# Weight remainders written over the loaded weight blocks: one ring of six slots, 74 pages, in a two-layer block stack on one core

## What is computed

```python
for l in range(DEPTH_2):
    h = rms_norm(x, ln_mix_pre[l])
    proj = h @ w_in[l]
    c_q, c_kv, k_pe, conv_u, r_q, r_k, r_v, r_g, gate_logits = jnp.split(proj, points, axis=-1)
    ...
    y_conv = conv_branch(conv_u, conv_w_dw[l], conv_b_dw[l], conv_ln_g[l], conv_ln_b[l], conv_w_pw[l])
    ...
    gates = jax.nn.sigmoid(gate_logits).reshape(B, S, N_BRANCH, D_MODEL)
    merged = gates[:, :, 0] * y_mla + gates[:, :, 1] * y_conv + gates[:, :, 2] * y_ret
    x = x + rms_norm(merged @ w_out[l], ln_mix_post[l])
    ...
def conv_branch(u, w_dw, b_dw, ln_g, ln_b, w_pw):
    a, gate = jnp.split(u, 2, axis=-1)
    a = a * jax.nn.sigmoid(gate)
    ...
    y = jax.nn.silu(layer_norm(y, ln_g, ln_b))
    return y @ w_pw
```

## Time and profile before

| | |
|---|---|
| median of 3 runs | 2887.31 us (2887.26 to 2887.69) |
| the profiled execution | 2887.51 us, its span 2885.5 us |
| granted TensorE clock, mean | 0.996 |
| PE busy | 2813.1 us, 97% of the span |
| DVE, ACT, POOL busy | 1284.7, 1136.1, 1193.7 us (45, 39, 41%) |
| DMA | 96 GB/s mean, 277.97 MB |

### The profile page before, as it was taken

One profiled execution on the slowest core, in us unless ns is written; L12 is line 12 of the kernel. 1 busy time (PEld: TensorE's weight loads), 2 busy tenths in 40 slices (PEclk: granted clock), 3 DMA queues, 4 the chain that ended last, 5 costly groups with the idle time before them and its releaser, 6 DMA issues.

```text
span 2885.5 us, 34416 instructions
## 1 busy us (share of the span) xinstructions
PE 2813.1 (97%) x13718; PEld 2245.5 (78%) x13718; DVE 1284.7 (45%) x1706; ACT 1136.1 (39%) x1687; POOL 1193.7 (41%) x539
## 2 busy tenths in 40 slices
PE   7999999999999999999999999999999999999999
PEld 6778778888888776787788888867757868788887
DVE  4776424611113867735315202277677353341123
ACT  4334643432233555433334322245555233443222
POOL 2123234354443662453444444436625434344442
PEclk9999999999999999999999999999999999999999
DMA  7344223333333220222232323332202323333332
GB/s 257 117 145 136 78 81 109 105 111 101 95 95 126 81 66 30 73 95 74 88 124 81 102 92 98 96 108 76 66 30 81 95 66 104 98 106 95 95 95 80
DMA packets 89278, 277.97 MB, mean 96 GB/s; under 512 B 9952, under 2 KB 10272, under 8 KB 89120
## 3 DMA queue, kind: packets, MB, share of 16 engines
q1 hardware_dynamic: 89120, 275.78, 29.4%
HBM read 268.40 MB, written 7.34 MB: 96 GB/s over the span
## 4 chain that ended last, share of the span: by engine, by line
PE 89%; DVE 8%; ACT 2%; issue 1%; DMA 0%; SPq 0%; DVEq 0%; ACTq 0%
PE bank L1684 23%; PE bank L1686 23%; PE bank L1685 23%; PE bank L2010 2%; PE bank L1817 2%; PE bank L1960 1%; PE bank L1734 1%; PE bank L1733 1%; PE bank L1735 1%; PE bank L1710 1%; PE bank L1972 1%; PE bank L1702 1%; PE bank L1703 1%; PE bank L2001 1%; DVE pageF L2819 1%
## 5 line engine op out<-in xcount | busy, mean ns | idle before, releaser
L2957 POOL TENSOR_TENSOR wlo<-wraw,whi 128x1024 fp32r<-128x1024 f32 x429 | 1042.8, 2433 | 1479.9 <-ACT whi L2039 1465.3
L1684 PE MATMUL bank<-pageR,whi 128*128 128x512 f32 x3184 | 1286.0, 404 | 6.4 <-ACT pageF L2292 1.6
L1686 PE MATMUL bank<-pageR,wlo 128*128 128x512 f32 x3184 | 1230.8, 387 | 0.0
L1685 PE MATMUL bank<-pageR,whi 128*128 128x512 f32 x3184 | 1229.6, 386 | 0.0
L1684 PEld LDWEIGHTS bank<-pageR,whi 128*128 128x128 f32 x3184 | 599.6, 188 | 158.8 <-issue 40.1
L1685 PEld LDWEIGHTS bank<-pageR,whi 128*128 128x128 f32 x3184 | 599.9, 188 | 135.7 <-issue 22.8
L1686 PEld LDWEIGHTS bank<-pageR,wlo 128*128 128x128 f32 x3184 | 599.0, 188 | 123.8
L2039 ACT ACTIVATE whi<-wraw 128x1024 fp32r<-128x1024 f32 x429 | 450.9, 1054 | 411.9 <-PE bank L1686 320.2
L2113 ACT ACTIVATE pageR<-pageF 128x512 fp32r<-128x512 f32 x136 | 86.1, 633 | 423.8 <-DVE pageF L2678 188.7
L2819 DVE SCALAR_TENSOR_TENSOR pageF<-pageF,prm 128x497 f32<-128x497 f32 (+9 forms) x180 | 189.5, 1053 | 2.5
L2966 POOL TENSOR_TENSOR pageR<-pageF,pageR 128x512 fp32r<-128x512 f32 x46 | 66.2, 1447 | 141.2 <-ACT pageR L2113 105.6
(11 more groups left out here) (236 smaller groups left out, 2609.4 us busy)
## 6 DMA issues: line engine op xcount, KB each, us to landing
wraw<-in_wst SPq DMA_DIRECT2D x429, 512.0 KB, 3.5
pageF<-in_wmod SPq DMA_DIRECT2D x96, 256.0 KB, 4.7
pageF<-in_xT SPq DMA_DIRECT2D x16, 256.0 KB, 4.1
pageF<-in_bias SPq DMA_DIRECT2D x16, 256.0 KB, 3.9
kept<-pageF SPq DMA_DIRECT2D x16, 256.0 KB, 4.7
pageF<-kept SPq DMA_DIRECT2D x16, 256.0 KB, 4.0
out_x<-pageF SPq DMA_DIRECT2D x8, 256.0 KB, 2.0
pageF<-in_cT SPq DMA_DIRECT2D x4, 256.0 KB, 10.1
```

The source lines that it names most:

```text
L1684: e.matmul(o, hi, xh, start=first, stop=False)
L1685: e.matmul(o, hi, xl, start=False, stop=False)
L1686: i = e.matmul(o, lo, xh, start=False, stop=last)
L2957: e.tensor_tensor(wlo[:, b % NH, :, :], wraw[:, b % NR, :, :], bc(whi[:, b % NH, :, :]), ALU.subtract).then_inc(*wlod.up(("wlo", b)))
```

## The change

The loaded blocks and the remainders share one ring of NL = 6 slots: the remainder of a block is written over the loaded block, in place. The high parts keep their ring of 4. The load of b now waits for `wdone` of b - 6 alone, and it is put on the list by the split of block b - 2 (before, by that of b - 3; the first three as before). The split on POOL no longer waits for `wdone` itself (ACT's high part, for which it waits, does). `mm_turned` cuts a product where either ring wraps; each of its 62 steps starts at a multiple of four slots, so that no product is cut in either kernel. Three slots of `wraw` and four of `wlo` become six, and NPAGE goes from 70 to 74.

```diff
@@ -18,8 +18,8 @@
 FT = 22
 FH = 11
 NB = 429
-NR, NH = 3, 4
-NPAGE = 70
+NL, NH = 6, 4
+NPAGE = 74
 NLAND = 100
 MSC = float(96 ** -0.5)
 RSC = float(128 ** -0.5)
@@ -176,7 +176,7 @@
         if b < NB and b == self.split:
             self.split += 1
             self.step("w_split", b)
-            self.w_load(b + NR)
+            self.w_load(b + (3 if b < 3 else 2))
 
     def w_slot(self, key):
         self.order.append(key)
@@ -1460,9 +1460,10 @@
             with nc.sbuf_tensor(f"pageF{i}", [128, 512], F32) as t:
                 pageF.append(t)
             pageR.append(sb(f"pageR{i}", [128, 512], F32R))
-        wraw = sb("wraw", [128, NR, 8, 128])
+        with nc.sbuf_tensor("wraw", [128, NL, 8, 128], F32) as wraw:
+            pass
+        wlo = sb("wlo", [128, NL, 8, 128], F32R)
         whi = sb("whi", [128, NH, 8, 128], F32R)
-        wlo = sb("wlo", [128, NH, 8, 128], F32R)
         prm = sb("prm", [128, NPC])
         cst = sb("cst", [128, 5, 128])
         with nc.sbuf_tensor("tabG", [128, 1792], F32) as tabG:
@@ -1484,7 +1485,7 @@
         whid, acp, fun = (Signal(sem(n), at) for n in ("s_whi", "s_copied", "s_function"))
         vec = Signal(sem("s_vector"), at)
         wlod, low = (Signal(sem(n), at) for n in ("s_wlo", "s_pool"))
-        raw = [Signal(sem(f"s_raw{i}"), at) for i in range(NR)]
+        raw = [Signal(sem(f"s_raw{i}"), at) for i in range(NL)]
         land = [Signal(sem(f"s_land{i}"), at) for i in range(NLAND)]
         stored = Signal(sem("s_stored"), at)
         counting = [True]
@@ -1585,10 +1586,9 @@
                 load(F(name) if dst is None else dst, src, *name)
 
             def w_load(b):
-                if b >= NR:
-                    w.wait_ge(*when("whi", b - NR))
-                    w.wait_ge(*when("wlo", b - NR))
-                e.dma_start(wraw[:, b % NR, :, :], a["wst"][b]).then_inc(*landed(raw[b % NR], "wraw", b))
+                if b >= NL:
+                    w.wait_ge(*when("wdone", b - NL))
+                e.dma_start(wraw[:, b % NL, :, :], a["wst"][b]).then_inc(*landed(raw[b % NL], "wraw", b))
 
             def load_fixed(name):
                 load(fixed[name], a[name], name)
@@ -1671,7 +1671,7 @@
 
             def mm(s, groups, first, last, final=True):
                 b, j = divmod(s, 8)
-                hi, lo = whi[:, b % NH, j, :], wlo[:, b % NH, j, :]
+                hi, lo = whi[:, b % NH, j, :], wlo[:, b % NL, j, :]
                 w.wait_ge(*when("whi", b))
                 w.wait_ge(*when("wlo", b))
                 for n, (name, x) in enumerate(groups):
@@ -1700,7 +1700,7 @@
                     if first:
                         clear(name)
                     e.matmul(bank(name), whi[:, b % NH, j, :], xh, start=first, stop=False)
-                    e.matmul(bank(name), wlo[:, b % NH, j, :], xh, start=False, stop=False)
+                    e.matmul(bank(name), wlo[:, b % NL, j, :], xh, start=False, stop=False)
 
             def mm_second_part(slots, outs, x, last):
                 xl = half(x, "lo")
@@ -1715,8 +1715,8 @@
                         i.then_inc(*lin.up(*names))
 
             def mm_turned(s, n, outs, x, first, last, final):
-                a, ring = s % (8 * NH), 8 * NH
                 hi, lo = (y[:, :, :, :].rearrange("p b j f -> p (b j) f") for y in (whi, wlo))
+                cuts = sorted({0, n, *(c for ring in (8 * NH, 8 * NL) for c in [ring - s % ring] if c < n)})
                 for b in range(s // 8, (s + n - 1) // 8 + 1):
                     w.wait_ge(*when("whi", b))
                     w.wait_ge(*when("wlo", b))
@@ -1726,13 +1726,12 @@
                     if first:
                         clear(name)
                     xh, xl = (half(x, part)[:, 128 * t:128 * t + 128] for part in ("hi", "lo"))
-                    for c, d in ((0, min(n, ring - a)), (ring - a, n)):
-                        if c < d:
-                            o, at0 = bank(name)[:, 128 * c:128 * d], (a + c) % ring
-                            h, r = hi[:, at0:at0 + d - c, :], lo[:, at0:at0 + d - c, :]
-                            e.matmul(o, xh, h, start=first and c == 0, stop=False, skip_group_check=True)
-                            e.matmul(o, xl, h, start=False, stop=False, skip_group_check=True)
-                            i = e.matmul(o, xh, r, start=False, stop=last and d == n, skip_group_check=True)
+                    for c, d in zip(cuts, cuts[1:]):
+                        o, h0, l0 = bank(name)[:, 128 * c:128 * d], (s + c) % (8 * NH), (s + c) % (8 * NL)
+                        h, r = hi[:, h0:h0 + d - c, :], lo[:, l0:l0 + d - c, :]
+                        e.matmul(o, xh, h, start=first and c == 0, stop=False, skip_group_check=True)
+                        e.matmul(o, xl, h, start=False, stop=False, skip_group_check=True)
+                        i = e.matmul(o, xh, r, start=False, stop=last and d == n, skip_group_check=True)
                     names = [name] if last else []
                     if final and t == outs[-1][0]:
                         names += [("wdone", b) for b in range(s // 8, (s + n) // 8)]
@@ -2036,7 +2035,7 @@
                 w.wait_ge(*when("wraw", b))
                 if b >= NH:
                     w.wait_ge(*when("wdone", b - NH))
-                e.activation(whi[:, b % NH, :, :], wraw[:, b % NR, :, :], ACT.Copy).then_inc(*whid.up(("whi", b)))
+                e.activation(whi[:, b % NH, :, :], wraw[:, b % NL, :, :], ACT.Copy).then_inc(*whid.up(("whi", b)))
 
             def square(t, i, src, c0, width, need, scale):
                 x = (F(src) if src in p.pages.place else bank(src))[:, c0:c0 + width]
@@ -2950,11 +2949,9 @@
                     w.wait_ge(*when(*k))
 
             def w_split(b):
-                if b >= NH:
-                    w.wait_ge(*when("wdone", b - NH))
                 w.wait_ge(*when("wraw", b))
                 w.wait_ge(*when("whi", b))
-                e.tensor_tensor(wlo[:, b % NH, :, :], wraw[:, b % NR, :, :], bc(whi[:, b % NH, :, :]),
+                e.tensor_tensor(wlo[:, b % NL, :, :], wraw[:, b % NL, :, :], bc(whi[:, b % NH, :, :]),
                                 ALU.subtract).then_inc(*wlod.up(("wlo", b)))
 
             def halves(x, src, made, lane):
```

## The result

Four runs of the changed kernel have a median of **2901.64 us** (2899.37 to 2903.68), four of the kernel before beside them 2887.50 (2887.26 to 2887.78): a ratio of 1.0050, 95% interval 1.0038 to 1.0062. The change makes the kernel slower by 14 us, 0.5%. The forecast was 2906, range 2896 to 2912.

What follows compares the result with a forecast made beforehand. The prediction took PE, busy 97% of the span, as the bound. Per layer it set a loss of 11.5 us against a gain of 2.2: 2 x (11.5 - 2.2) = + 18.6 us on 2887.5, so 2906, range 2896 to 2912.

Steps and rivals of the forecast that it cites:

- The ring itself: Weight blocks: the later load is covered by 7 us of PE's work per block, so cost 0.
- The order is the change: Two places per layer: a 2.2 us gain at attention's end, an 11.5 us loss at the convolution branch's norm.
- Fourth page at T + 16.5: Convolution norm: the fourth page's remainder ends 16.5 us after T, bounds 14.2 and 18.3.
- T: Start of the convolution norm's square sum on PE, 1218.45 us in the profile before.
- Product at T + 17.5, + 9.5 us: Convolution branch: `w_pw`'s first product ends at about T + 17.5, against T + 8.0 before; 9.5 us added per layer.
- Clock behind the wait, + 2 us: After PE's long wait at the convolution norm, the lowered clock loses 2 us per layer, bounds 0 and 3.
- Gain at the end of attention, 2.2 us: Four gates between attention's steps make 11.19 us of PE time cost 9.0: 2.2 us gained per layer, bounds 0 and 5.1.
- The empty yield saved at `main_ret(1)`: One empty yield fewer at `main_ret(1)` touches nothing that PE waits for; put at nothing.
- A shorter wait with a richer cover: Rival: smallest loss at the convolution norm and largest gain at attention's end, + 3.6 us, 2891; chance 0.06.
- late loads: Rival: where transfers crowd, PE waits for a weight's remainder, ten waits of 1 us on top, 2916; chance 0.06.
- a ring in effect waiting: Rival: each block's load in effect waits for PE, over 1 us a block, 400 us and more; chance under 0.01.
- the room only removes bubbles: Rival: convolution branch ready by its product, so only attention's gain remains, 2 x 2.2 us, 2883; chance 0.06.

Runs made afterwards that it cites:

- the ring alone: The changed kernel with 70 pages instead of 74, so PE's instructions keep the order of the kernel before; 2886.5 us, ratio 0.9999 to the kernel before.
- the order alone with the old rings: The kernel before with 72 pages and both free-page thresholds lowered by two, giving PE the changed kernel's instruction order; 2903.5 us, ratio 1.0061 to the kernel before.
- matmuls in the wait: The changed kernel plus eight matmuls of constants, result unread, between the convolution branch's last gate projection ahead and its first product needing the norm; 2902.4 us.
- five gates ahead: The changed kernel with up to five gate projections ahead in the convolution branch instead of four; 2894.5 us, ratio 1.0032 to the kernel before.
- remainders on VectorE: The changed kernel with the four remainders of the normed convolution pages computed on VectorE instead of GpSimd; 2916.0 us, ratio 1.0101 to the kernel before.
- the kernel without the four gates: The changed kernel with 74 pages, its attention branch running a gate ahead only with 12 free pages, so none; 2891.2 us, ratio 1.0016 to the kernel before.
- seven gates ahead: The changed kernel with seven gate projections ahead in the convolution branch, 84 matmuls of cover; 2881.4 us, ratio 0.9983 to the kernel before.

## Why the prediction was right, and where its sizes were off

- **The ring itself, cost 0**: right. Shown by the ring alone (ratio 0.9999), and the in-place subtraction measured 2.42 us. A slot less did no harm either.
- **The order is the change, with two places**: right, shown by the order alone with the old rings. The two new idle times came as described, each once in a layer, released by L2963. They were 8.6 us, longer than the 6 to 8 I had named. Of the shorter ones that I expected behind them there is one, 0.20 us in layer 1; they appear where the clock is up (0.34 us with matmuls in the wait). The idle times ahead of the values of head pair 2 are gone, and the two waits of 2.1 us at the square sum are the same.
- **Fourth page at T + 16.5**: it came at T + 16.1. The parts: the delay ahead of the logarithm was + 2.3, as worked out; from the logarithm to the first SiLU - 0.7 (I had - 0.6); from there to the last remainder - 1.5 (I had - 1.2), from 8.1 to 6.6 us. ACT's two steps took 1.28 us a page and not the sum of their durations, 1.36. DVE's four steps took 2.73 us, 0.68 each, instead of 7.00, now that no subtraction of POOL runs beside them. The rule of the Trainium skill on which I had leant ("SBUF — State Buffer", section SBUF: two separate sides, on the shared port pair) fits these rows, and the trace with five gates ahead bears it out more closely: of four such steps in a row only the one that fell beside a subtraction was long, and it ended half a microsecond after it.
- **Product at T + 17.5, + 9.5 us**: T + 17.04, + 9.0.
- **Clock behind the wait, + 2 us**: this is the step that failed. It is 0, shown by keeping the clock up: the product and the milestone behind it didn't move. I had taken the price of the idle time at 84.86 us, behind which PE has work in hand. Here PE is fed at the pace of the pages, which is just that of the lower clock, and the clock is back for the last page. That the fall behind T would lie under the wait needed no answer: there was none in the changed kernel's execution. In the experiment with remainders on VectorE the two microseconds do appear, because there the clock is still low behind the last page.
- **Gain at the end of attention, 2.2 us**: net 1.3 to 1.5, and over a third of it at the retention's square sum, which I had not looked at. I had put 1.2 of the 2.2 down to idle time and 1.0 to steps that are cheaper between projections; what was gained is nearly all idle time. The empty yield saved at `main_ret(1)`, which I had put at nothing, costs 1.3 in the kernel without the four gates: it moved the retention projections one step up and so out from under the attention's end. How much of this the gates make good again is not separated. That is the other step that failed, and it fell against the gain.
- **The sum**: 2 x (9.0 - 1.5) = + 15 instead of + 18.6, and the medians differ by 14.1. From 18.6 to 15 it is 4 for the clock and 0.9 for the product's end, less 1.4 for the smaller gain, so the errors offset one another in part; the last microsecond is within the spread of the runs.
- **The rivals.** A shorter wait with a richer cover, late loads and a ring in effect waiting did not happen. That the room only removes bubbles, by the rule of the Trainium skill ("Perfetto Trace Analysis", where it stands in section Optimization Strategy), was wrong for the kernel as changed; but with the norm's cover restored the same room did make it faster (seven gates ahead, 0.17% [0.09, 0.26%]).

## What to carry to other kernels

More room in a planned kernel is not only fewer waits for room: it changes the order, and each piece of work taken forward to fill one gap is taken from another. Before giving buffers to such a planner, list the chains that it covers by accident (here a norm of 16 us behind one square sum) and fix their cover in the code, by a least number of independent matmuls behind the step that starts the chain. And when a step is moved to a faster engine, look at what stands behind it on that engine's list: in order, a wait for another engine's answer stops the run-ahead of all that follows.

## What the hardware showed that I had not expected

- The same idle time of 2.13 us ahead of the same instruction is followed by the lower clock in some executions and not in others (0.57 and 1.00 behind the two square sums of one execution). A fall cost 1.6 or 1.7 us. The kernel before had given 2887.26 to 2887.78 us in four runs, but over one group of 21 runs it ranged from 2882.9 to 2889.3. Falls of this kind are a likely source. They were seen only in single profiles, but the mean granted clock of each run points the same way: in the second group of 21, the nine runs under 2886 us all have 0.996, and the seven from 2888.5 to 2889.3 all have 0.994.
- A clock at its lower level may cost nothing at all, where the supply of pages is as slow as that.
- A DVE step with two SBUF operands on 128x512 took 0.68 us each in a row of four while POOL was idle, and 1.75 us each beside POOL's subtractions (one weight block and the page remainders). A single one that fell beside the subtraction of a weight block took 2.84 us.
